# Norm sums of the hybrid layers: from fp32 products per tile to one high and low pair per sum

## The reference, cut to what matters

```python
def rms_norm_2(x, g):
    xf = x.astype(jnp.float32)
    y = xf * lax.rsqrt(jnp.mean(xf * xf, axis=-1, keepdims=True) + NORM_EPS)
    return (y * g.astype(jnp.float32)).astype(x.dtype)

def layer_norm(x, g, b):
    mu = jnp.mean(xf, axis=-1, keepdims=True)
    xc = xf - mu
    var = jnp.mean(xc * xc, axis=-1, keepdims=True)
    y = xc * lax.rsqrt(var + NORM_EPS) * g + b
...
    q = (rms_norm_2(b_qlat, g_q_lat) @ w_uq)         # latent of 256 channels
    kv = (rms_norm_2(b_kvlat, g_kv_lat) @ w_ukv)     # latent of 128 channels
...
    u = lax.conv_general_dilated(u, w_dw, ...) + b_dw   # 31 taps, 256 channels
    out_d = jax.nn.silu(layer_norm(u, g_conv_ln, b_conv_ln))
```

## Time and profile before

| | |
|---|---|
| median of 3 runs | 2792.51 us (2792.32 to 2792.86) |
| the profiled execution | 2792.07 us |
| its span in the trace | 2790.3 us |
| PE busy | 2772.5 us (99%) |
| PEld busy | 2261.4 us (81%) |
| DVE busy | 1245.8 us (45%) |
| ACT busy | 1241.7 us (45%) |
| POOL busy | 1225.5 us (44%) |
| granted TensorE clock | 0.998 of full speed |

### The profile page before, as it was taken

One profiled execution on the slowest core, in us unless ns is written; L12 is line 12 of the kernel. 1 busy time (PEld: TensorE's weight loads), 2 busy tenths in 40 slices (PEclk: granted clock), 3 DMA queues, 4 the chain that ended last, 5 costly groups with the idle time before them and its releaser, 6 DMA issues.

```text
span 2790.3 us, 32430 instructions
## 1 busy us (share of the span) xinstructions
PE 2772.5 (99%) x12950; PEld 2261.4 (81%) x12950; DVE 1245.8 (45%) x2087; ACT 1241.7 (45%) x1813; POOL 1225.5 (44%) x545
## 2 busy tenths in 40 slices
PE   9999999999999999999999999999999999999998
PEld 8876888888888888887777888888877778888887
DVE  4676551544675435327666432021266674420112
ACT  4665442444864334334774343143246744442331
POOL 3222444444554444443555444444434564444443
PEclk9999999999999999999999999999999999999999
DMA  4222332333233323332222323333322223233332
GB/s 153 91 69 62 97 100 90 105 99 93 89 98 102 100 91 100 98 98 84 69 76 84 106 91 98 98 98 97 100 91 77 68 84 98 91 98 99 98 98 76
DMA packets 74726, 259.25 MB, mean 93 GB/s; under 512 B 9856, under 2 KB 9856, under 8 KB 74576
## 3 DMA queue, kind: packets, MB, share of 16 engines
q1 hardware_dynamic: 73280, 255.08, 29.3%
q10 hardware_dynamic: 1296, 2.10, 0.2%
HBM read 254.95 MB, written 2.13 MB: 92 GB/s over the span
## 4 chain that ended last, share of the span: by engine, by line
PE 96%; DVE 2%; ACT 1%; DMA 0%; issue 0%; POOL 0%; SPq 0%; DVEq 0%; ACTq 0%
PE ps L463 28%; PE ps L465 28%; PE ps L464 28%; PE ps L539 2%; PE ps L570 2%; PE ps L553 1%; PE ps L596 1%; PE ps L598 1%; PE ps L597 1%; PE ps L474 1%; PE ps L519 1%; PE ps L521 1%; PE ps L520 1%; ACT pbuf L1023 0%; ACT w_hi L963 0%
## 5 line engine op out<-in xcount | busy, mean ns | idle before, releaser
L2074 POOL TENSOR_TENSOR w_lo<-raw,w_hi 128x1024 fp32r<-128x1024 f32 x469 | 1130.6, 2413 | 1482.8 <-ACT w_hi L963 1482.6
L463 PE MATMUL ps<-xs,w_hi 128*128 128x512 f32 x2176 | 861.7, 396 | 1.6 <-DVE xs L1464 1.6
L465 PE MATMUL ps<-xs,w_lo 128*128 128x512 f32 x2176 | 847.1, 389 | 0.0
L464 PE MATMUL ps<-xs,w_hi 128*128 128x512 f32 x2176 | 847.0, 389 | 0.0
L963 ACT ACTIVATE w_hi<-raw 128x1024 fp32r<-128x1024 f32 x470 | 494.6, 1054 | 637.6 <-PE ps L465 601.2
L463 PE MATMUL ps<-hid,w_hi 128*128 128x512 f32 x1316 | 514.5, 391 | 0.0
L465 PE MATMUL ps<-hid,w_lo 128*128 128x512 f32 x1316 | 512.2, 389 | 0.0
L464 PE MATMUL ps<-hid,w_hi 128*128 128x512 f32 x1316 | 512.1, 389 | 0.0
L463 PEld LDWEIGHTS ps<-xs,w_hi 128*128 128x128 f32 x2176 | 408.5, 188 | 96.2 <-issue 8.3
L464 PEld LDWEIGHTS ps<-xs,w_hi 128*128 128x128 f32 x2176 | 408.6, 188 | 88.6 <-issue 5.2
L465 PEld LDWEIGHTS ps<-xs,w_lo 128*128 128x128 f32 x2176 | 408.5, 188 | 85.5
(11 more groups left out here) (234 smaller groups left out, 2571.6 us busy)
## 6 DMA issues: line engine op xcount, KB each, us to landing
raw<-in_weights SPq DMA_DIRECT2D x470, 512.0 KB, 3.5
btab<-in_rel SPq DMA_DIRECT2D x8, 256.0 KB, 4.1
out<-tmp ACTq DMA_DIRECT2D x8, 256.0 KB, 2.0
hT<-in_x SPq DMA_DIRECT2D x3, 512.0 KB, 7.0
btab<-in_heads SPq DMA_DIRECT2D x6, 256.0 KB, 4.0
tmp<-in_heads SPq DMA_DIRECT2D x6, 256.0 KB, 3.9
common<-in_fixed SPq DMA_DIRECT2D x1, 642.0 KB, 10.3
hT<-in_x SPq DMA_DIRECT2D x2, 256.0 KB, 4.0
```

Source lines behind the costliest of these rows:

```text
L463: pe.matmul(banks[bank][:], wh, rh, start=(k == 0), stop=False)
L464: pe.matmul(banks[bank][:], wh, rl, start=False, stop=False)
L465: last = pe.matmul(banks[bank][:], wl, rh, start=False, stop=(k == len(specs) - 1))
L2074: gp.tensor_tensor(w_lo[:, n % NPAIR, :], raw[:, n % NRAW, :], w_hi[:, n % NPAIR, :].bitcast(F32), ALU.subtract).then_inc(*w_low.tick(n))
```

## The change

Two tiles whose sums are to be added are added on VectorE first, the total is split into a high and a low part, and TensorE makes two fp32r passes with a constant matrix in fp32r. `latent_squares` is a new step between `latent` 2 and `c_head` 0; `conv_sum` is a new step in front of `gated` (2, 2); `conv_square`, which only ScalarE had (in front of `gated` (2, 3)), now has VectorE's part too. A wait on `low` replaces the waits on `squared`, `taps` and `pool` on TensorE.

```diff
+        means = sb("means", [P, 2, P], F32R)
...
-        before2 = [("latent", 0), ("by_token", 0), ("latent", 1), ("latent", 2), ("c_head", 0), ("latent_norms", 0),
+        before2 = [("latent", 0), ("by_token", 0), ("latent", 1), ("latent", 2), ("latent_squares", 0), ("c_head", 0), ("latent_norms", 0),
...
-            steps2 += [("conv_square", 0)] if c == 1 else []
-            steps2 += [("gated", (2, 2 + c)), (what, 0)]
+            steps2 += [[("conv_sum", 0)], [("conv_square", 0)], [], []][c] + [("gated", (2, 2 + c)), (what, 0)]
...
+        lat_squares = [(att[:, 11, :], (hid[:, 12, :], hid[:, 11, :])), (att[:, 13, :], (hid[:, 14, :], hid[:, 13, :]))]
+        con_sum, con_parts = att[:, 20, :], (hid[:, 16, :], hid[:, 17, :])
+        con_square, con_square_parts = tmp[:, 1, :], (hid[:, 18, :], hid[:, 19, :])
... TensorE
-                        for which, (lhs, parts) in enumerate(((one256, (0, 1)), (one128, (2,)))):
+                        for which, lhs in enumerate((mean256, mean128)):
                             bk = next_bank(("latent_norm", L, which))
-                            for n in parts:
-                                T.wait_ge(squared, ("latent", L, n))
+                            T.wait_ge(low, ("latent", L, which))
                             wait_bank(bk)
-                            sum_over(bk, ("latent", L, which), lhs, [att[:, 11 + n, :] for n in parts])
+                            sum_over(bk, ("latent", L, which), lhs, lat_squares[which][1])
...
-                        T.wait_ge(taps, ("conv", L, 0, 30))
-                        T.wait_ge(pool, ("conv", L, 1, 30))
+                        T.wait_ge(low, ("conv_sum", L))
                         wait_bank(4)
-                        sum_over(4, ("conv_mean", L), one256, [dcon[:, 0, :], dcon[:, 1, :]])
+                        sum_over(4, ("conv_mean", L), mean256, con_parts)
...
-                        for c in range(2):
-                            T.wait_ge(squared, ("conv", L, c))
+                        T.wait_ge(low, ("conv_square", L))
                         wait_bank(0)
-                        sum_over(0, ("conv_var", L), one256, [tmp[:, 1, :], tmp[:, 2, :]])
+                        sum_over(0, ("conv_var", L), mean256, con_square_parts)
... ScalarE
+                    elif what == "latent_squares":
+                        for which, (total, parts) in enumerate(lat_squares):
+                            if which == 0:
+                                A.wait_ge(summed, ("latent", L))
+                            else:
+                                A.wait_ge(squared, ("latent", L, 2))
+                            take_high(parts[0], total, ("latent", L, which))
...
+                    elif what == "conv_sum":
+                        A.wait_ge(summed, ("conv_sum", L))
+                        take_high(con_parts[0], con_sum, ("conv_sum", L))
                     elif what == "conv_square":
                         for c in range(2):
                             A.wait_ge(vec, ("centred", L, c))
                             ac.activation(tmp[:, 1 + c, :], dcon[:, c, :], ACT.Square).then_inc(*squared.tick(("conv", L, c)))
+                        A.wait_ge(summed, ("conv_square", L))
+                        take_high(con_square_parts[0], con_square, ("conv_square", L))
... VectorE
-            ve.memset(ones[:, 1, :], 1.0 / 256)
             ve.memset(ones[:, 2, :], 1.0 / 128)
+            ve.memset(mean256.bitcast(F32), 1.0 / 256)
+            ve.memset(mean128.bitcast(F32), 1.0 / 128)
...
+                    elif what == "latent_squares":
+                        for n in range(2):
+                            V.wait_ge(squared, ("latent", L, n))
+                        ve.tensor_tensor(att[:, 11, :], att[:, 11, :], att[:, 12, :], ALU.add).then_inc(
+                            *summed.tick(("latent", L)))
+                        for which, (total, parts) in enumerate(lat_squares):
+                            take_low(parts, total, ("latent", L, which))
...
+                    elif what == "conv_sum":
+                        V.wait_ge(taps, ("conv", L, 0, 30))
+                        V.wait_ge(pool, ("conv", L, 1, 30))
+                        ve.tensor_tensor(con_sum, dcon[:, 0, :], dcon[:, 1, :], ALU.add).then_inc(*summed.tick(("conv_sum", L)))
+                        take_low(con_parts, con_sum, ("conv_sum", L))
+                    elif what == "conv_square":
+                        for c in range(2):
+                            V.wait_ge(squared, ("conv", L, c))
+                        ve.tensor_tensor(con_square, tmp[:, 1, :], tmp[:, 2, :], ALU.add).then_inc(
+                            *summed.tick(("conv_square", L)))
+                        take_low(con_square_parts, con_square, ("conv_square", L))
```

More of the change, by code:

```diff
@@ L165, in program @@
         ropec = common[:, 1280:1284]
-        one1024, one256, one128, one1 = (ones[:, i, :] for i in range(4))
+        one1024, one128, one1 = (ones[:, i, :] for i in (0, 2, 3))
+        mean256, mean128 = means[:, 0, :], means[:, 1, :]
         eps = tiny[:, 0:1]
```

## The result

| | before | after |
|---|---|---|
| median of 9 runs each | 2792.32 us (2791.6 to 2792.86) | 2785.23 us (2783.95 to 2786.43) |
| span of the profiled execution | 2790.3 us | 2783.6 us |
| ratio of the runs | | 0.9975 (95%: 0.9966 to 0.9984) |

A forecast was written before the change was run, and what follows sets the result against it. PE was taken to bound the kernel, busy 99% of the span. Work gained, 8.62 us, less 2 x 0.13 and 2 x 0.55 of stalls gave 7.26 us, so 2785.2 us, range 2783.2 to 2787.2.

The forecast's parts named there:

- The work: PE sums in each hybrid layer: fp32 halves of 6.12 us become eight fp32r passes of 1.81, gaining 4.31 us per layer.
- The bank at `c_head` 1: PE waits for bank 5, which DVE empties, after the four latent passes: 0.13 us per layer, bounds 0 and 0.4.
- The mean: At the mean sum the new add and split are hidden, slack 1.9 us; ACT's slab copy goes later without starving PE.
- The variance: POOL's later subtraction holds DVE's accumulator add, so PE stalls 0.55 us per layer before the variance sum.
- the fork: With the skill's rule the variance add is held 0.72 us longer, gain 7.26 us; without it 8.36.
- The sum: Whole kernel: 8.62 - 2 x 0.13 - 2 x 0.55 = 7.26 us gained, median 2785.2 us.
- Start: One more memset of 0.14 us before the first matmul costs nothing, at most 0.14 us.
- B: Rival: no stall worth naming at either restart; gain 8.4 to 8.6 us, 2784.0 us; chance 0.25.
- C: Rival: one more POOL subtraction before the new add or low at `conv_square`, both layers; gain 2.5, 2790.0 us; chance 0.06.
- D: Rival: passes with the fp32r constant run like fp32 halves; 2787.3 us, or 2788.7 if stalls stay; chance 0.06.
- E: Rival: slower through slab starvation at `conv_sum`, PE having 3.3 us to spare; 2795.3 us at 9 us late; chance 0.03.
- A: Likeliest case: the gain as summed, with both stalls; 2785.2 us, own range 2784.4 to 2786.4; chance 0.60.

The follow-up runs named there:

- own banks: The whole change, but the two latent sums go to banks 0 and 1 instead of two of the ring of three; 2784.41 us in one execution.
- the kernel with both edits: The whole change plus banks 0 and 1 for the latent sums and conv_var one gated group later; 2782.92 us, ratio to before 0.9966.
- the run with the copy ahead of the high: The whole change, but in conv_square ACT copies the slab of gate (2, 3) before waiting for the add of the squares; 2792.34 us in one execution.
- the kernel with 0.16 us at the mean: The whole change, but ACT copies the slab of gate (2, 2) before waiting for conv_sum's add; 2785.74 us in one execution.

## Why the prediction was right

- **The work.** 4.31 us per layer, from the starts in the earlier trace rows, against 4.32 with both waits gone (score to score). The start-to-start price was right; the mean of 590 ns in the earlier trace rows would have given 14 x 0.59 - 8 x 0.39 = 5.1.
- **The bank at `c_head` 1.** Forecast 0.13 us, measured 0.21 (own banks). PE resumed 0.92 us after the start of DVE's scale (1245.02 to 1245.94, taken back from the next pass), where 0.84 had been taken from the earlier trace rows.
- **The mean.** No wait, as forecast; the new add started with the end of the old one and took 0.68.
- **The variance.** Forecast 0.55 us, measured 0.66. The chain ran as worked out: the accumulator add took 2.38 us (forecast 2.4), the low started at 1508.67, the weight load 0.74 after it at 1509.41. Without the wait the pass's place is 1509.53 - 0.64 = 1508.89, so 0.64 was lost at the wait; 0.02 more went in the passes behind it, which start 0.23 apart for a while. Of the miss, 0.07 lies in one link: VectorE's add of the squares started 0.73 us after ScalarE's second square (at 1507.28 and 1506.54), where 0.66 had been taken from a pair of high and low in the earlier trace rows. The Trainium skill's rule on two SBUF inputs ("SBUF — State Buffer", section "Who interferes with whom") gave the right side of the fork. The two runs with a slab copy moved agree with it: with POOL ahead the new add took 2.88 us and the low 2.43, and without it 0.68 and 0.69.
- **The sum.** Per layer 4.31 forecast less 0.68, measured 3.44 = 4.31 less 0.87. The two waits together were taken 0.19 us too short per layer (0.08 at the bank, 0.11 at the variance), 0.4 in all; that is the mis-sized term. In the median it doesn't show: 2785.23 against 2785.2 us is closer than the working was, and that is luck. Score to score gives 2 x 3.44 = 6.9 us of gain where 7.26 was forecast, and a later set of seven runs of the same kernel has a median of 2784.46 us.
- **Start.** One memset more moved the first warm-up matmul from 1.48 to 1.62 us. What of it reaches the end wasn't separated. The wait that ended at 12.79 ended at 12.95 after the change, but at 12.63 in its second execution, and the latent sums of the two executions lay 1.8 us apart.
- **Rivals.** B (no stall) is out as such, but is what the kernel with both edits does. C (one more subtraction in front of the low) did not happen in the change; the run with the copy ahead of the high brought it about, with 788.39 us from score to score. Its price of 2.4 would give 787.4; the wait grew by 1.75 only, and the clock's 1.6 comes on top. D is out: passes with the new constant are 0.227 apart. E did not happen; ACT's late copy cost PE nothing. The slab in question had more to spare than E gave it: by the count of passes (18 behind the mean) PE opened it at 1506.17, and POOL was done with it at 1502.41, so 3.8 us and not 3.3.
- **The chances.** They don't add up as written: A and B are 0.85 together, so with their upper ends left out they are less than that and not 0.87, and C and D alone are 0.12 and not 0.10.

## What to carry to other kernels

Price PE work by the distance between starts, and then ask of each product that gets shorter whose work it had been covering: here two late chains came out from behind the fp32 halves. A VectorE instruction with two SBUF inputs that starts while a GpSimd subtraction runs can be held until that has ended: in the cases above 0.69 us alone became 1.16 to 2.88 us, each ending 0.55 us after GpSimd's recorded end. Whether it happens followed from the order in which ScalarE's queue released GpSimd. Moving the consumer one step back in the order took the wait at the variance away whole; changing the order inside the chain only moved the long instruction. A faster chain was not tried.

## What the runs showed of the hardware that had not been expected

- The held instruction is no special case of this chain. In the trace of the kernel before, 41 tensor_tensors of VectorE with both inputs in SBUF start while a subtraction of GpSimd runs, and 38 of them end 0.54 to 0.64 us after its recorded end, with lengths up to 2.90 us; one, at 800.97, took 0.68 us and was not held. The 184 with an input in PSUM that start under the same condition all took 0.67 to 0.70 us. So the price of such an instruction could be counted before the change was built.
- After 2.11 us of idle time in the middle of dense work, TensorE ran eight passes at the lower of its clocks, in both layers: 1.6 us more each. After 0.37 us of idle time at the same place the granted clock was 1.00 in both windows, from 1505 to 1510 and from 1510 to 1515 us; it was also 1.00 in each of the three windows from 1500 to 1515 us in the kernel with 0.16 us at the mean.
- At the very end of the program the last eight 128-column matmuls took 2.05 us in the change (granted clock 0.58 over 3 us from 2773) and 1.15 us in the kernel that adds without splitting (0.89 over 3 us from 2774). That kernel's span is 0.8 us longer than the change's, where score to score has 2 x 0.84 = 1.7. The change's second execution has 1.50 us in the same row. So a difference of 1 or 2 us between kernels is better read between two places in the middle than from the span. The rows, in the order named:

```profile
2773.62 2.05 PE L951 MATMUL ps<-tmp,ones 128*128 128x128 f32 x8 [0.98 <-DVE tmp L2092]
2775.34 1.15 PE L951 MATMUL ps<-tmp,ones 128*128 128x128 f32 x8 [0.98 <-DVE tmp L2077]
2771.79 1.50 PE L951 MATMUL ps<-tmp,ones 128*128 128x128 f32 x8 [0.98 <-DVE tmp L2092]
```
